# One broadcast matmul from doubled gate rows, and a last projection with the tokens on the partitions

## The chip, the cores and the metric

The program runs on one core of a Trainium2 chip. The metric is the device time of one execution in microseconds (us), from runs of the whole kernel; lower is better.

## The reference

Input and output are 512 tokens of 1024 features, all in float32. The first block normalises the tokens, projects them onto some 13,000 columns and feeds three branches: HGRN2 (8 heads), a stabilised mLSTM (4 heads) and Mamba-2 (16 heads in 4 groups). Each branch is multiplied by a sigmoid gate and its own output matrix, the sum goes through `w_out`, and a gated feed-forward layer with a short convolution follows. The second block has a gated convolution and a windowed attention of 8 heads. Two places matter for the change. In the mLSTM and in Mamba-2, rows over time enter an exponential for every pair of tokens t, s (here of Mamba-2):

```
cum = moveaxis(cumsum(dtc * A, axis=1), 1, 2)
L = exp(where(tri, cum[..., :, None] - cum[..., None, :], NEG_BIG))
y_intra = einsum('bhts,bshp->bthp', CB * L, xdt)
```

So a row of 512 numbers, one per token, has to stand on all partitions. The other place is the very end:

```
y = concatenate([y_conv, y_attn], axis=-1)
x = x + einsum('bse,ed->bsd', y, w_out)
return x
```

Here `y` has 4 tiles of 128 features from the convolution (numbers 0 to 3) and 4 from the attention (4 to 7).

## The kernel before

**Layout.** Activations lie with features on the partitions: a tile is 128 features by 512 tokens, and 8 tiles are the whole width. TensorE, the tensor engine, works on float32r operands, float32 rounded so that a matmul takes one pass; to keep float32 accuracy each operand is split into a high and a low part, and a product is three matmuls (high·high, high·low, low·high; L397, L398 and L399 in `project`). Weights come in 245 slabs of 512 KB, eight 128 x 128 blocks each. SyncE (SP) loads a slab into one of four buffers (L331) when `slab_used` says that its predecessor there has been used; ScalarE (ACT) writes its high part (`slab_hi`, L855); GpSimd (POOL) writes the low part over the raw slab (`slab_lo`, L362) and counts `slab_split`, for which TensorE waits. `project` takes one slab: 24 matmuls of 128 x 512 into one of two accumulator banks of PSUM (`acc`), in turn.

**Order.** Every engine runs a list of instructions written out by hand and waits on counting semaphores. The stages follow one another: HGRN2, the gate rows, four mLSTM heads, four Mamba-2 groups, mixing, feed-forward, attention with the gated convolution, and the last projection. Inside a stage TensorE alternates projections for the next unit with the small matmuls of the present one.

**The broadcast (`on_all`, L403 to L407).** The rows (Mamba-2's 16 heads in rows 0 to 15, the mLSTM's i and f in rows 32 to 35 and 64 to 67) are computed by VectorE (DVE) in `rows_part`, beside the projections of the first gates. The last steps split the row tile `r3` into `csh` (high) and `csl` (low, L1476), and copy two selection matrices to `selr` (L1465, L1466). `on_all(bank, c, sem)` takes column c of `selr`, repeated 128 times as the stationary operand, and runs two matmuls of 128 x 512, one with `csh` and one with `csl`, so that one row stands on all partitions of a bank. It is called 24 times: per mLSTM head once ahead of the exponentials (part 0, bank 5) and once behind the numerators (part 2, bank 2), and once per Mamba-2 head (`mb_bcast`, bank 5).

**A Mamba-2 group.** TensorE: `mb_start` transposes two tiles, multiplies B and C, and ends with the broadcast of head 0, which waits until `mb_rms` has read bank 5. Then for h = 0 to 3: a projection for the next group, the broadcast of head h + 1 (h < 3), and behind h = 1 and h = 3 the values of two heads (`mb_values`, L618). Two projections and `mb_finish` follow. DVE works through: the last normalisation of the group before (L1772, two), two tiles times dt (L1750), then per head four additions (`mb_head`, L1734), a convolution of four steps for the next group (L1503, L1508; from head 1 on, and not in the last group), and three products (`mb_weights`, L1744). ACT has the exponentials between them (L1092, L1093).

**The last projection, J_O2 = 237.** Slab 237 + f holds the columns of output feature tile f for all 8 input tiles. The first projection runs six of its blocks (input tiles 0, 1, 2, 4, 5, 6), then TensorE turns the last two rows of attention weights (`at_turn`, L771), computes the last values (`at_values`, L782; it waits for `at_copy` on ACT, L1285) and runs blocks 3 and 7, which wait for the low halves of those tiles: `cv_lo` (L2012), and `at_end`, `at_hi`, `at_lo` (L1972, L1289, L1977). DVE adds each finished bank to the residual `xT` (L2048); one projection later `turn_out` transposes the sum's four blocks (L833), ACT copies them (L1351) and SP stores them (L346): 128 features of all tokens, in runs of 512 bytes. Behind the last projection this chain stands alone. ACT's list there is `cv_silu`, two `at_copy`, `cv_hi`, `at_hi`, slab 240, then one slab and one copy in turn.

## Time and profile before

| | |
|---|---|
| Median of 3 runs | 1667.75 us (1667.38 to 1668.54) |
| The profiled execution's own time | 1668.24 us |
| Its span, first to last instruction | 1666.4 us |
| Instructions | 21787 |

A row of the timeline has the start in us, the duration (of the whole group, where it has several), the engine, the line of the kernel, the operation, output and inputs by name, shapes and count, and in brackets how long the engine sat idle and what released it. PEld is the loading of a stationary operand, PE the matmul. A matmul's duration is longer than the distance to the next start, since matmuls overlap; the distance is what it costs.

### The profile page before, as it was taken

How to read it: one execution, taken by the hardware profiler on the slowest of the kernel's cores; microseconds unless marked ns; L12 is line 12 of the kernel's file. 1: busy time of each engine (PE TensorE's matmuls, PEld its weight loads, DVE VectorE, ACT ScalarE, POOL GpSimd, SP SyncE). 2: the span in 40 equal slices, each digit the busy share in tenths (PEclk: the TensorE clock that was granted, in tenths of full speed). 3: DMA queues.
4: the chain of work that ended last, by engine and by line, in shares of the span. 5: the costliest groups of instructions: out<-in, count | busy, mean ns of one | idle time of the engine just before them, and what ended most of it. 6: DMA issues, size and time to landing. Idle time of an engine off the chain costs nothing.

```text
span 1666.4 us, 21787 instructions
## 1 busy us (share of the span) xinstructions
PE 1626.3 (98%) x7802; PEld 1303.4 (78%) x7802; DVE 855.5 (51%) x1329; ACT 723.4 (43%) x1143; POOL 607.8 (36%) x254
## 2 busy tenths in 40 slices
PE   7999999999999999999999999999999999999889
PEld 6888888777877778777777878888888877777667
DVE  4788878532454551167643335444443335565651
ACT  4656665332344432354554344444343333435441
POOL 5333223343333334332233434444444443242222
PEclk9999999999999999999999999999999999999999
DMA  5222112122222223222222322323233352222112
GB/s 185 65 64 64 63 63 64 54 88 89 87 76 76 66 75 101 76 76 64 64 76 82 95 89 93 96 89 99 88 101 102 101 178 88 64 76 68 59 51 89
DMA packets 41785, 139.31 MB, mean 84 GB/s; under 512 B 4200, under 2 KB 8552, under 8 KB 41712
## 3 DMA queue, kind: packets, MB, share of 16 engines
q1 hardware_dynamic: 40080, 132.66, 25.3%
q10 hardware_dynamic: 1632, 5.64, 0.9%
q8 instruction: 51, 0.84, 0.2%
q14 instruction: 22, 0.18, 0.0%
HBM read 136.15 MB, written 2.13 MB: 83 GB/s over the span
## 4 chain that ended last, share of the span: by engine, by line
PE 87%; DVE 6%; ACT 3%; issue 3%; DMA 0%; DVEq 0%; ACTq 0%; SPq 0%
PE bank L397 25%; PE bank L398 25%; PE bank L399 25%; PE bank L491 2%; PE bank L618 1%; PE bank L782 1%; PE bank L762 1%; DVE s_p L1744 1%; PE bank L771 1%; DVE unit L1508 1%; DVE hgd L1525 1%; DVE s_e L1734 0%; PE bank L588 0%; PE bank L508 0%; PE bank L539 0%
## 5 line engine op out<-in xcount | busy, mean ns | idle before, releaser
L362 POOL TENSOR_TENSOR wl<-raw,wh 128x1024 fp32r<-128x1024 f32 x245 | 599.6, 2449 | 1028.0 <-ACT wh L855 1027.7
L397 PE MATMUL bank<-hh,wh 128*128 128x512 f32 x968 | 390.2, 403 | 1.4 <-DVE hl L1977 1.0
L398 PE MATMUL bank<-hl,wh 128*128 128x512 f32 x968 | 382.9, 396 | 0.0
L399 PE MATMUL bank<-hh,wl 128*128 128x512 f32 x968 | 382.8, 395 | 0.0
L397 PE MATMUL bank<-yh,wh 128*128 128x512 f32 x800 | 320.9, 401 | 0.7 <-DVE yl L1779 0.5
L398 PE MATMUL bank<-yl,wh 128*128 128x512 f32 x800 | 317.0, 396 | 0.0
L399 PE MATMUL bank<-yh,wl 128*128 128x512 f32 x800 | 316.9, 396 | 0.0
L855 ACT ACTIVATE wh<-raw 128x1024 fp32r<-128x1024 f32 x241 | 253.2, 1054 | 110.8 <-DMA raw<-slabs 110.8
L397 PEld LDWEIGHTS bank<-hh,wh 128*128 128x128 f32 x968 | 182.1, 188 | 47.0 <-issue 4.1
L399 PEld LDWEIGHTS bank<-hh,wl 128*128 128x128 f32 x968 | 182.0, 188 | 44.3
L398 PEld LDWEIGHTS bank<-hl,wh 128*128 128x128 f32 x968 | 182.3, 188 | 42.0 <-issue 0.7
L397 PEld LDWEIGHTS bank<-yh,wh 128*128 128x128 f32 x800 | 150.8, 189 | 42.9 <-issue 6.2
L399 PEld LDWEIGHTS bank<-yh,wl 128*128 128x128 f32 x800 | 150.8, 189 | 36.7
L398 PEld LDWEIGHTS bank<-yl,wh 128*128 128x128 f32 x800 | 150.9, 189 | 35.5 <-issue 0.5
L1863 DVE TENSOR_TENSOR f_t<-bank,rsn 128x512 f32<-128x512 f32 x44 | 30.4, 692 | 121.5 <-PE bank L399 115.6
L397 PE MATMUL bank<-fh,wh 128*128 128x512 f32 x176 | 69.6, 396 | 0.0
L398 PE MATMUL bank<-fl,wh 128*128 128x512 f32 x176 | 69.6, 396 | 0.0
L399 PE MATMUL bank<-fh,wl 128*128 128x512 f32 x176 | 69.6, 396 | 0.0
L1525 DVE TENSOR_TENSOR hgd<-hg 128x512 f32<-128x512 f32 x56 | 67.2, 1200 | 0.0
L1834 DVE TENSOR_TENSOR xT<-xT,bank 128x512 f32<-128x512 f32 x16 | 11.0, 688 | 102.2 <-PE bank L399 102.2
L1331 ACT ACTIVATE a_l<-a_l,a_st 128x512 f32<-128x512 f32 x32 | 23.2, 725 | 88.7 <-DVE a_st L1956 88.7
L491 PEld LDWEIGHTS bank<-hgz 128*128 128x128 f32 x448 | 53.6, 192 | 7.8 <-issue 3.8
(304 smaller groups left out, 1874.7 us busy)
## 6 DMA issues: line engine op xcount, KB each, us to landing
raw<-slabs SPq DMA_DIRECT2D x245, 512.0 KB, 3.5
wb<-bias_scratch ACTq DMA_DIRECT2D x1, 3584.0 KB, 12.4
xs<-x SPq DMA_DIRECT2D x4, 512.0 KB, 6.1
out<-htn SPq DMA_DIRECT2D x8, 256.0 KB, 2.3
con<-consts ACTq DMA_DIRECT2D x1, 992.5 KB, 4.7
oneh<-onehot ACTq DMA_DIRECT2D x1, 512.0 KB, 5.6
con<-consts ACTq DMA_DIRECT2D x1, 192.0 KB, 4.6
par<-params ACTq DMA_DIRECT2D x1, 191.5 KB, 6.1
```

Source lines behind the costliest of these rows:

```text
L362: pool.tensor_tensor(slab(wl, i), slab(raw, i), slab(wh, i).bitcast(F32), ALU.subtract).then_inc(S["slab_split"], 1)
L397: mm(bank[:, :], wh[:, s, b, :], xh, start=first and i == 0, stop=False)
L398: mm(bank[:, :], wh[:, s, b, :], xl, start=False, stop=False)
L399: ins = mm(bank[:, :], wl[:, s, b, :], xh, start=False, stop=last and i == len(order) - 1)
L491: ins = mm(bank[:, b * P // 2:(b + 1) * P // 2], blk(z, b), right[:, b, :, :], start=True, stop=True)
L618: ins = mm(bank[64 * v:64 * v + 64, o:o + n], s_x[:, b, h + v, :], s_p[v][:, a:a + n], start=k == 0, stop=k == len(parts) - 1)
L762: ins = mm((b5, b6)[hd][:, :], a[r, q * P:(q + 1) * P], b[r, :], start=k == 0, stop=k == 2)
L771: ins = pe.transpose(blk((b2, b3)[i % 2], b), blk(a_l[i % 4], b), ident)
L855: A(wh[:, i].rearrange("p k f -> p (k f)"), raw[:, i].rearrange("p k f -> p (k f)"), ACT.Copy).then_inc(S["slab_hi"], 1)
L1331: A(a_l[i % 4][:, :], a_l[i % 4][:, :], ACT.Exp, bias=a_st[:, i, 0:1], accum_out=a_st[:, i, 1:2]).then_inc(S["at_ex"], 1)
L1525: TT(o, v, v[:, :, half - 1:half].broadcast_to([P, T // n, n]), ALU.subtract).then_inc(S["hg_d"], 1)
L1863: TT(f_t[v][:, :], acc[j0 % 2][:, :], rsn[:, :], ALU.mult).then_inc(acc_free[j0 % 2], 1)
```

## The change

Three things are changed.

**Doubled rows.** The gate weights' slab, their biases and constants hold each gate row a second time, 16 rows further down. DVE's last step makes one tile `cs`: its first copies hold -r3, its second copies the difference of the high part and r3. A selection column has -1 at both copies, so that one matmul sums both. The low part `csl`, the second selection matrix and the second matmul of `on_all` go. DVE has one small copy less.

**Token-major last projection.** The stationary operand is now a 128 x 128 block of `hh` or `hl` (128 tokens), the moving one two rows of a slab with 512 output columns. A slab holds two input tiles for half of the output columns. Per half (g) and block of 128 tokens (b), one bank takes first the four transposed residual tiles and then the 24 matmuls of four slabs on top. The order of the input tiles is (0, 1), (2, 4), (5, 6), (3, 7). TensorE runs: tile (0, 0); `at_turn` of rows 6 and 7; tile (0, 1); `at_values`; tile (0, 2); the wait for the last low halves; tile (0, 3); tiles (1, 0) to (1, 3).

**Leaving.** `turn_out` and DVE's additions are gone. ACT copies the banks of token blocks 0 and 2, DVE those of blocks 1 and 3, straight from PSUM, and SP stores each in runs of 2048 bytes. ACT does slab 240 ahead of `cv_hi` and `at_hi`.

```diff
             def on_all(bank, c, sem):
 
                 w = selr[:, c:c + 1].broadcast_to([P, P])
-                mm(bank[:, :], w, csh[:, :], start=True, stop=False)
-                mm(bank[:, :], w, csl[:, :], start=False, stop=True).then_inc(sem, 1)
+                mm(bank[:, :], w, cs[:, :], start=True, stop=True).then_inc(sem, 1)
...
-                    dve.tensor_copy(selr[:, 0:P], ident).then_inc(S["rnm_done"], 1)
-                    dve.tensor_copy(selr[:, P:2 * P], cc(K_SEL2)).then_inc(S["rnm_done"], 1)
+                    dve.tensor_copy(selr[:, :], cc(K_SEL2)).then_inc(S["rnm_done"], 1)
...
-                    TT(csl[:, :], r3[:, :], csh[:, :].bitcast(F32), ALU.subtract).then_inc(S["rnm_done"], 1)
+                    STT(cs[:, :], csh[:, :].bitcast(F32), cc(K_AGAIN, 1), r3[:, :], ALU.mult, ALU.subtract
+                        ).then_inc(S["rnm_done"], 1)
...
-            project(J_O2, src=(hh, hl), t0=J_O2 - DN_SHIFT, order=(0, 1, 2, 4, 5, 6), last=False,
-                    ready=[(sem, i) for sem in (S["cv_lo"], S["at_lo"]) for i in (1, 2, 3)])
+            def out_tile(g, i):
+
+                j = J_O2 + 4 * g + i
+                pe.wait_ge(S["slab_split"], j + 1)
+                w = [t[:, j % 4].rearrange("p k f -> p (k f)") for t in (wh, wl)]
+                for b in range(NB):
+                    bank = out_banks[g][b]
+                    if i == 0:
+                        out_free(g, b)
+                        for f in range(4):
+                            mm(blk(bank, f), blk(xT[:, 4 * g + f, :], b), ident, is_transpose=True, start=f == 0,
+                               stop=False)
+                    for n, k in enumerate(O2_PAIRS[i]):
+                        xh, xl = blk(hh[:, k, :], b), blk(hl[:, k, :], b)
+                        for c, (v, u) in enumerate(((xh, 0), (xl, 0), (xh, 1))):
+                            ins = mm(bank[:, :], v, w[u][:, n * T:(n + 1) * T], start=False,
+                                     stop=i == 3 and n == 1 and c == 2)
+                    if b == NB - 1:
+                        ins.then_inc(S["slab_used"], 1)
+                    elif i == 3:
+                        ins.then_inc(S["out_sum"], 1)
+
+            out_banks = ((acc[1], acc[0], b4, b5), (b6, b2, b3, b7))
...
+            out_tile(0, 0)
             at_turn(6, 3)
             at_turn(7, 3)
+            out_tile(0, 1)
             at_values(3, 3)
...
+            out_tile(0, 2)
+            pe.wait_ge(S["cv_lo"], 4)
+            pe.wait_ge(S["at_lo"], 4)
+            out_tile(0, 3)
+            for i in range(4):
+                out_tile(1, i)
...
+            slab_hi(J_O2 + 3)
             cv_hi(3)
             at_hi(3)
-            slab_hi(J_O2 + 3)
...
+            for g in range(2):
+                for b in (0, 2):
+                    act.wait_ge(S["out_sum"], 3 * g + b + 1)
+                    A(os_[g][b], (acc[1], None, b4, None, b6, None, b3)[4 * g + b][:, :], ACT.Copy
+                      ).then_inc(S["out_ev0"], 1)
+                    if g == 0 and b == 0:
+                        slab_hi(J_O2 + 7)
...
+            for g in range(2):
+                for b in (1, 3):
+                    if b == 3:
+                        dve.wait_ge(S["slab_used"], J_O2 + 4 * g + 4)
+                    else:
+                        dve.wait_ge(S["out_sum"], 3 * g + b + 1)
+                    dve.tensor_copy(os_[g][b], (None, acc[0], None, b5, None, b2, None, b7)[4 * g + b][:, :]
+                                    ).then_inc(S["out_ev1"], 1)
```

## Rows read from the trace of the kernel before

**Rows 1.** The page: busy time, and the shares of the chain that ended last.

```profile
PE 1626.3 (98%) x7802; PEld 1303.4 (78%) x7802; DVE 855.5 (51%) x1329; ACT 723.4 (43%) x1143; POOL 607.8 (36%) x254
...
PE 87%; DVE 6%; ACT 3%; issue 3%; DMA 0%; DVEq 0%; ACTq 0%; SPq 0%
```

**Rows 2.** Views of one line: L407 (ns least/median/most, first and last start), and L1362.

```profile
L407 PE MATMUL bank<-csl,selr x24: 388/392/400, 438.0 to 865.1; 128*128 128x512 f32 x24
...
L1362 DVE COPY xT<-bank x6: 682/685/692, 6.6 to 11.2; 128x512 f32<-128x512 f32 x6
```

**Rows 3.** Timeline, PE: a broadcast in group 1 of Mamba-2, and the values behind one in group 3.

```profile
762.43 0.40 PE L406 MATMUL bank<-csh,selr 128*128 128x512 f32 x1
762.66 0.39 PE L407 MATMUL bank<-csl,selr 128*128 128x512 f32 x1
763.57 1.63 PE L618 MATMUL bank<-s_p,s_x 128*64 128x384 f32 x14 [0.52 <-DVE s_p L1744]
...
856.81 0.87 PE L618 MATMUL bank<-s_p,s_x 128*64 128x384 f32 x4
```

**Rows 4.** Busy time by stretch (start:end, length, then each engine; PEclk the granted clock).

```profile
320.00:560.00 240.00, 240.00 (x1093) 192.88 (x1093) 97.62 (x145) 83.88 (x118) 83.99 (x36) 1.00 0.26 79
699.00:702.60 3.60, 3.09 (x15) 3.12 (x16) 1.38 (x2) 2.69 (x4) 0.00 (x0) 0.53 0.23 88
1576.00:1583.00 7.00, 6.21 (x20) 4.39 (x18) 5.91 (x12) 3.17 (x6) 2.38 (x1) 0.52 0.00 0
```

**Rows 5.** Timeline, mLSTM head 0: DVE's last sum, TensorE's first value matmul.

```profile
455.52 0.29 DVE L1690 TENSOR_TENSOR m_ps<-m_ps,m_p 128x128 f32<-128x128 f32 x1
...
458.07 0.81 PE L584 MATMUL bank<-m_p,m_v 128*128 128x384 f32 x2
```

**Rows 6.** Timeline, DVE in group 1, from the normalisation's end to its second products.

```profile
750.19 1.41 DVE L1772 SCALAR_TENSOR_TENSOR s_y<-s_y,par,s_rs 128x512 f32<-128x512 f32 x2 [6.22 <-ACT s_rs L1112]
...
761.91 1.60 DVE L1744 TENSOR_TENSOR s_p<-s_e,bank 128x512 f32<-128x512 f32 x3
```

**Rows 7.** Timeline, DVE: group 0, then head 3 of group 1, then group 3.

```profile
710.76 1.13 DVE L1734 SCALAR_TENSOR_TENSOR s_e<-bank,ncc,con 128x128 f32<-128x128 f32 x4 [1.07 <-PE bank L407]
...
772.26 1.13 DVE L1734 SCALAR_TENSOR_TENSOR s_e<-bank,ncc,con 128x128 f32<-128x128 f32 x4 [2.93 <-PE bank L407]
...
854.99 1.62 DVE L1744 TENSOR_TENSOR s_p<-s_e,bank 128x512 f32<-128x512 f32 x3 [2.25 <-ACT s_e L1093]
```

**Rows 8.** Timeline around the last attention values.

```profile
1608.74 0.50 PE L397 MATMUL bank<-hh,wh 128*128 128x512 f32 x1
...
1615.39 1.09 PE L782 MATMUL bank<-a_pt,a_v 128*64 128x128 f32 x16 [1.32 <-ACT a_pt L1285]
...
1618.69 0.50 PE L397 MATMUL bank<-hh,wh 128*128 128x512 f32 x1 [1.03 <-DVE hl L1977]
```

**Rows 9.** Timeline, the end: last matmul, transposes, the last sum, its way out.

```profile
1661.09 0.39 PE L399 MATMUL bank<-hh,wl 128*128 128x512 f32 x1
1661.32 0.60 PE L833 MATMUL bank<-con,xT 128*128 128x128 f32 x4
1661.64 0.69 DVE L2048 TENSOR_TENSOR xT<-xT,bank 128x512 f32 x1 [5.34 <-PE bank L399]
...
1662.58 1.49 SPq L346 DMA_DIRECT2D out<-htn  x2
1663.07 0.60 ACT L1351 ACTIVATE htn<-bank 128x512 f32<-128x512 f32 x1 [0.52 <-PE bank L833]
```

**Rows 10.** DMA issues of the page: KB each, median us from issue to landing.

```profile
raw<-slabs SPq DMA_DIRECT2D x245, 512.0 KB, 3.5
out<-htn SPq DMA_DIRECT2D x8, 256.0 KB, 2.3
```

**Rows 11.** Timeline, PE: a transpose group between two projections; float32 matmuls over a sum.

```profile
1655.28 0.60 PE L833 MATMUL bank<-con,xT 128*128 128x128 f32 x4
...
462.45 1.02 PE L591 MATMUL bank<-m_ps,con 128*128 128x512 f32 x2
```

More of the change, by code:

```diff
@@ L86 @@
 ROW_DT, ROW_I, ROW_F = 0, 32, 64
+AGAIN = 16
 W_BIAS = 896
@@ L311, in build @@
         rr, a_y = sqn
-        os_ = htn
+        os_ = [[t[:, :] for t in a_l], [au[0][:, b, :] for b in range(NB)]]
         OFF = {0: (512, 384), 2: (896, 128), 1: (1024, 256)}
@@ new lines, in _, with out_free @@
+            out_banks = ((acc[1], acc[0], b4, b5), (b6, b2, b3, b7))
+            def out_free(g, b):
+                if b == 0 and g == 0:
+                    pe.wait_ge(S["x2_done"], 9)
+                    pe.wait_ge(acc_free[1], (J_O2 - DN_SHIFT) // 2)
+                elif b == 1 and g == 0:
+                    pe.wait_ge(acc_free[0], (J_O2 - DN_SHIFT + 1) // 2)
+                elif b == 2 and g == 0:
+                    pe.wait_ge(S["at_v"], 4)
+                elif b == 3 and g == 0:
+                    pe.wait_ge(S["at_l"], 32)
@@ L822, in _ @@
+            out_tile(0, 0)
             at_turn(6, 3)
             at_turn(7, 3)
+            out_tile(0, 1)
             at_values(3, 3)
-            project(J_O2, src=(hh, hl), t0=J_O2 - DN_SHIFT, order=(3, 7), first=False,
-                    ready=[(S["cv_lo"], 4), (S["at_lo"], 4)])
-            def turn_out(f):
-                filled(pe, J_O2 - DN_SHIFT + f)
-                wait(pe, S["out_ev"], f - 3)
-                for b in range(NB):
-                    ins = pe.transpose(blk(psum[2 + f % 4], b), blk(xT[:, f, :], b), ident)
-                ins.then_inc(S["out_tr"], 1)
@@ L836, in _ @@
-            for f in range(1, KT):
-                project(J_O2 + f, src=(hh, hl), t0=J_O2 - DN_SHIFT + f)
-                turn_out(f - 1)
-            turn_out(KT - 1)
+            out_tile(0, 2)
[4 more added lines that the diff above has]
+                out_tile(1, i)
         @block.scalar
@@ L2041, in _ @@
             at_lo(3)
-            dve.wait_ge(S["x2_done"], 9)
-            with dve.Fori(0, KT // 4) as it:
-                for f in range(4):
-                    t = J_O2 - DN_SHIFT + f
-                    dve.wait_ge(S["slab_used"], it * 4 + (J_O2 + f + 1))
-                    fo = it * 4 + f
-                    TT(tile_of(xT, fo), tile_of(xT, fo), acc[t % 2][:, :], ALU.add).then_inc(acc_free[t % 2], 1)
+            for g in range(2):
+                for b in (1, 3):
[5 more added lines that the diff above has]
+                                    ).then_inc(S["out_ev1"], 1)
 def bucket(rel):
@@ L2066, in constants @@
     c[:, K_BD:K_BD + P] = (i[:, None] // AT_DH) == (i[None] // AT_DH)
-    for h in range(ML_HEADS):
-        c[ROW_I + h, K_SELI + ROW_I + h] = 1
-        c[ROW_I + h, K_SEL2 + h] = c[ROW_F + h, K_SEL2 + h] = 1
-        c[ROW_F + h, K_NSELF + ROW_I + h] = -1
+    for d in (0, AGAIN):
+        for h in range(MB_HEADS):
+            c[ROW_DT + d + h, K_SEL2 + ROW_DT + h] = -1
+        for h in range(ML_HEADS):
+            c[ROW_I + d + h, K_SELI + ROW_I + d + h] = 1
+            c[ROW_F + d + h, K_NSELF + ROW_I + d + h] = -1
+            c[ROW_I + d + h, K_SEL2 + ROW_I + h] = -1
+            c[ROW_I + d + h, K_SEL2 + ROW_F + h] = c[ROW_F + d + h, K_SEL2 + ROW_F + h] = -1
+    c[:, K_AGAIN] = i // AGAIN % 2
     c[:, K_CLAMP:K_CLAMP + P] = np.where(i[:, None] <= i[None], 0.0, NEG)
@@ L2103, in slabs_of @@
     for row, c, n in ((ROW_DT, C_MBDT, MB_HEADS), (ROW_I, C_MLIF, ML_HEADS), (ROW_F, C_MLIF + ML_HEADS, ML_HEADS)):
-        small[:, :, row:row + n] = w_in[:, c:c + n].reshape(KT, P, n).transpose(1, 0, 2)
+        for d in (0, AGAIN):
+            small[:, :, row + d:row + d + n] = w_in[:, c:c + n].reshape(KT, P, n).transpose(1, 0, 2)
     for u in range(HG_HEADS):
@@ L2122, in slabs_of @@
         put(J_O + f, i["w_out"][0], P * f)
-        put(J_O2 + f, i["w_out_2"], P * f)
         for c, n in enumerate(DN_CHUNKS):
             put(J_DN + 3 * f + c, w_dn, P * f, 8 * c, n)
+    for g in range(2):
+        for s, pair in enumerate(O2_PAIRS):
+            for n, k in enumerate(pair):
+                a[J_O2 + 4 * g + s].reshape(P, 2, T)[:, n] = i["w_out_2"][k * P:(k + 1) * P, g * T:(g + 1) * T]
     for j in range(NF):
```

50 lines of the change are left out of this document (23 added, 27 removed).

## The prediction

> **What bounds the kernel now.** I read the page first: TensorE is busy for 98% of the span, and the chain that ended last lies on it for 87% [rows 1]. Rows of single lines and of the timeline come next, because with such a share the question is not which engine bounds the kernel but where TensorE's list is what everybody waits for, and where it waits itself. In the busy times by stretch, 320 to 560 us, which holds mLSTM work, has TensorE busy for all of its 240 us [rows 4]: a matmul less there is time less. In Mamba-2 it is not always so: TensorE waits for DVE's products ahead of the values [rows 3]. At the end it waits twice around the last attention values [rows 8], and behind the last matmul a chain of DVE, TensorE, ACT and SP stands alone [rows 9].
>
> **The broadcast, unit price.** One matmul of 128 x 512 goes from each of 24 calls [rows 2]. It lasts 0.39 us, but the next one starts 0.23 us after it [rows 3], and this distance is what it occupies. All 24 are 5.5 us. A page's rule gives another price: the Trainium skill, "TensorE: Matmul & The Clock Gate", section "Back-to-back issue gap", has 512 / 2.4 + 2.5 = 216 ns for one. By it, 24 would be 5.2 us, and what I count below as 3.5 us would be 3.2. The trace disagrees, and its distance is used.
>
> **The broadcast in the mLSTM.** Eight calls. TensorE has no idle time there [rows 4], and the nearest wait has room: in head 0 DVE's last sum ends at 455.81, and the first value matmul starts at 458.07 [rows 5]. Two calls per head take less than 0.5 us out of that room of 2.3 us, and what follows a call starts earlier too. So 8 x 0.23 = 1.8 us.
>
> **The broadcast in Mamba-2, group by group.** In group 1, DVE goes from the end of the normalisation at 750.19 to its second products, which end at 761.91 + 1.60 = 763.51 [rows 6]. On the way it waits for ACT alone. TensorE issues three broadcasts in this time, and then waits for the products and starts at 763.57 [rows 3]. Three matmuls less bring TensorE there 0.7 us earlier, to the same wait: worth nothing, the idle 0.5 us becomes 1.2. Group 2 has the same list of work, so the same. In group 3, without convolutions, DVE's second products end at 854.99 + 1.62 = 856.61 [rows 7] and TensorE starts the values at 856.81 [rows 3]. With the 0.06 us that group 1 shows between end and start, 0.14 us is left to win of 0.7. In group 0 nothing of a group before holds DVE: it waits for the broadcast, at 710.76 [rows 7]. There broadcasts 0 and 1 count in full; of broadcast 2 I take 0.1, between 0 and 0.23. The fourth broadcast of every group counts, since DVE waits for it (2.93 us in group 1 [rows 7]), and TensorE and what it waits for move together. Mamba-2 is then 0.56 + 0 + 0 + 0.14 + 4 x 0.23 = 1.6 us. Both together give **3.5 us**. The ends are 1.8 (no more than the mLSTM) and 5.5.
>
> **The rows themselves.** The doubled columns use slab columns that the projection multiplies anyway; one step of DVE changes its form, and one copy goes. All of it lies beside projections in a stretch in which TensorE has no idle time [rows 4]: nothing. If that cover were gone, it would be a small copy gained.
>
> **The last projection, TensorE.** From 1608.74 to the transposes at 1661.32 are 52.6 us [rows 8, 9]. One projection and one group of four transposes take 1661.32 - 1655.28 = 6.04 us [rows 9, 11], of which 24 x 0.233 = 5.60 are matmuls and 0.44 transposes. Eight projections and the six groups within the stretch are 8 x 6.04 - 2 x 0.44 = 47.4 us; the two turns, eight transposes, are 0.9, the values (1.09 of duration [rows 8], less the overlap) 1.0. That leaves 52.6 - 49.3 = 3.3 us in which TensorE waits or refills, of which the rows name 1.32 and 1.03. The new order puts 5.6 us of matmuls between the turns and the values, and again between the values and the wait for the last low half. Before, that second wait ends 1618.69 - 1616.48 = 2.2 us behind the values [rows 8]: 5.6 covers it, even with a slab ahead of `cv_hi` on ACT, which only delays a tile that is needed a whole out tile later. I take 3.0 of the 3.3 us, and 0.3 stays as refill. Against it stand 0.87 us: all 32 transposes are now ahead of the last matmul, before only 24. Number and distance of the matmuls stay: blocks of 128 x 128 stationary, 512 columns moving, both ways. So the last matmul starts 2.1 us earlier.
>
> **The way out.** Before, from the last matmul at 1661.09: DVE starts 0.55 later, adds for 0.69, TensorE turns, ACT copies until 1663.07 + 0.60 = 1663.67 [rows 9]. Now DVE copies from PSUM, 0.685 us [rows 2], and is done 0.55 + 0.69 = 1.24 behind it instead of 2.58: 1.3 us. The last store is of 256 KB as before; it took 2.3 us to land, and a slab, twice as large in runs eight times as long, 3.5 [rows 10]. Longer runs then give between nothing and 0.55 us (half of a slab's time, as if there were no fixed part); I take nothing, because the out row itself is the nearest. By the Trainium skill ("DMA: Bandwidth & Descriptors", "Why small descriptors are slow"), each packet costs three cycles beside its 32-byte beats; by that the move to 2048 bytes would save some 0.1 us, not shown by any row here.
>
> **Supply and queues.** SP's list has the same slabs; slab 241 may be loaded when tile (0, 0) is done, which is earlier than before, and is needed 18 us later. ACT's slabs 241 to 243 sit behind `at_hi`, and its first copy behind slab 243; that copy delays only stores of the first half, with 20 us left. DVE has nothing else. The banks that tile (0, 0) takes are free by the time it comes to them: the last is bank 5, which DVE reads for two logits, of about the 0.69 us of its addition [rows 9] each with a reduction between, while blocks 0 to 2 take 3 x (0.44 + 6 x 0.233) = 5.5 us. The end is worth 2.1 + 1.3 = **3.5 us** (rounded once).
>
> **Sum.** 3.5 + 3.5 = 6.9 us with the decimals kept. The profiled execution took 1668.24 us with a span of 1666.4; it becomes 1661.3. It lies 0.5 us above the median, so from the median of 1667.75 I say **1660.8**.
>
> **Rivals.** The difference from no change that a measurement of this kernel can tell is 0.2%, 3.3 us.
>
> *All broadcasts count.* If DVE's chain in Mamba-2 shortened as well, 5.5 in place of 3.5: 1658.8. Against it, the chain of group 1 waits for nothing of TensorE's [rows 6]. 8%.
>
> *The end keeps its stalls.* If the order or a bank held TensorE as before: 3.0 less, 1663.8. For it, out tile (0, 0) now waits for two more banks; against it, their readers are done. 6%.
>
> *No broadcast counts*, since other waits take their place in the mLSTM and in group 0 too: 1664.3. Against it, the full 240 us [rows 4]. 8%.
>
> *The clock.* TensorE was granted half its 2.4 GHz, 1.2 GHz, in two places: 0.53 on average of 3.6 us behind its wait at the start of Mamba-2, and 0.52 over 7 us behind the waits in the attention [rows 4]. Group 1 and 2 now wait 1.2 us instead of 0.5. One more stretch like the first costs 3.6 x 0.47 = 1.7 us: 1662.5. Against it, waits of 1.3 us did not bring the clock down at 1615 [rows 8]: TensorE's distances stay at 0.23 behind it. 9%.
>
> *Nothing visible*, no broadcast counts and the stalls stay: 1667.3. That the change doesn't do what it says ends here too, if the doubled rows only shifted the waits. 5%.
>
> *Slower: the matmuls of the last projection take longer.* Its place is the 192 matmuls onto a bank that a transpose has opened, with the weights as the moving operand. From 6.9 / 192 = 0.036 us more for each, the gain is gone. The nearest dearer row is float32 matmuls of the same shape, two in 1.02 us of duration [rows 11], some 0.43 each, 0.20 more: 192 x 0.20 = 38 us, 1699. Against it, both operands stay float32r, and a matmul behind transposes keeps its distance but for the 0.44 counted. 3%.
>
> **How the numbers follow.** My forecast has 61%, and the predicted time is its own. The range is to hold 8 in 10: forecast, all broadcasts, the clock and the stalls, with 0.6 us to both sides for the scatter of the runs (1667.38 to 1668.54). It is 1658.2 to 1663.9, and leaves out the three others, 16%. Faster by over 0.2% (below 1664.4) are the forecast and the first four rivals: 0.92. Within 0.2%: 0.05. Slower: 0.03.
>
> **What would show it.** Right: 24 rows of one broadcast matmul; the first values of groups 1 and 2 still start 13.4 us behind the normalisation's end, with 1.2 us idle ahead; no wait above 0.3 us from 1608 on; the last copy ends 1.2 us behind the last matmul's start. Wrong: idle time in the mLSTM stretch, a distance other than 0.233 us in the last projection, a wait for a slab there, or a stretch with a lower clock where there was none.

## The result, and the profile after

| | before | after |
|---|---|---|
| median of 5 runs, us (lowest to highest) | 1667.38 (1664.79 to 1668.54) | 1657.11 (1656.43 to 1659.72) |
| profiled execution, us (span; mean granted clock) | 1668.24 (1666.4; 0.994) | 1656.43 (1654.4; 0.997) |

The ratio is 0.9944, with a 95% interval of 0.9932 to 0.9955: faster by over 0.2%, as forecast, but 1657.11 is 3.7 us under the number and 1.1 us under the range of the forecast.

The page of the kernel after: busy times and the chain, to be held against [rows 1], then the two stores of the output, against [rows 10].

```profile
PE 1617.4 (98%) x7778; PEld 1296.2 (78%) x7778; DVE 854.2 (52%) x1324; ACT 721.7 (44%) x1139; POOL 605.9 (37%) x254
...
PE 87%; DVE 6%; ACT 3%; issue 3%; DMA 0%; DVEq 0%; ACTq 0%; SPq 0%
...
out<-a_l SPq DMA_DIRECT2D x4, 256.0 KB, 4.1
out<-au SPq DMA_DIRECT2D x4, 256.0 KB, 2.0
```

TensorE has 24 matmuls less, the chain is where it was. The stores of the first half land behind slab traffic in 4.1 us, which nobody waits for; those of the second half in 2.0 us, before 2.3.

Timeline of TensorE in groups 1 and 3 of Mamba-2, against [rows 3], and of DVE in group 1, against [rows 6].

```profile
757.70 0.40 PE L408 MATMUL bank<-cs,selr 128*128 128x512 f32 x1
759.18 1.08 PE L619 MATMUL bank<-s_p,s_x 128*64 128x384 f32 x6 [1.08 <-DVE s_p L1773]
...
851.84 0.87 PE L619 MATMUL bank<-s_p,s_x 128*64 128x384 f32 x4 [0.35 <-DVE s_p L1773]
```

```profile
745.79 1.42 DVE L1801 SCALAR_TENSOR_TENSOR s_y<-s_y,par,s_rs 128x512 f32<-128x512 f32 x2 [6.21 <-ACT s_rs L1139]
```

From the start of the normalisation's last step (which the forecast calls its end) to the first values it is 759.18 - 745.79 = 13.39 us; before 763.57 - 750.19 = 13.38. Three matmuls of the broadcasts are gone in between, and TensorE waits 1.08 us instead of 0.52; the forecast had 1.2.

Busy time by stretch (columns as in [rows 4]).

```profile
320.00:560.00 240.00, 240.00 (x1093) 192.90 (x1092) 97.18 (x144) 84.21 (x118) 85.09 (x36) 1.00 0.25 79
697.00:700.60 3.60, 3.19 (x23) 2.90 (x24) 1.29 (x2) 2.59 (x4) 0.00 (x0) 1.00 0.20 79
1569.80:1576.80 7.00, 7.00 (x38) 5.20 (x37) 6.07 (x12) 3.19 (x6) 2.41 (x1) 0.76 0.00 0
```

The mLSTM still has no idle time. But the second stretch has the full clock, where [rows 4] had 0.53, and the third 0.76 instead of 0.52. That is not a matter of instructions: r1_after below has the same ones, and a low clock there.

Timeline of the end, in two pieces: the last turns and the subtraction in DVE that was late before; the last values, and the last matmul with its way out, against [rows 8, 9].

```profile
1601.71 0.48 PE L836 MATMUL bank<-wh,hh 128*128 128x512 f32 x1
...
1608.66 1.04 PE L772 MATMUL bank<-con,a_l 128*128 128x128 f32 x8
...
1611.88 2.48 DVE L2041 TENSOR_TENSOR hl<-c,hh 128x512 fp32r<-128x512 f32 x1 [4.23 <-ACT hh L1324]
```

```profile
1614.82 0.40 PE L836 MATMUL bank<-wl,hh 128*128 128x512 f32 x1
1615.14 1.09 PE L783 MATMUL bank<-a_pt,a_v 128*64 128x128 f32 x16
1616.16 0.51 PE L836 MATMUL bank<-wh,hh 128*128 128x512 f32 x1
...
1650.84 0.40 PE L836 MATMUL bank<-wl,hh 128*128 128x512 f32 x1
1651.27 0.69 DVE L2077 COPY au<-bank 128x512 f32<-128x512 f32 x1 [2.06 <-PE bank L836]
1651.99 0.33 SPq L350 DMA_DIRECT2D out<-au  x1
```

Both waits of [rows 8] are gone, and the last copy ends 1651.96 - 1650.84 = 1.12 us behind the last matmul's start. DVE's low half took 2.48 us, beside POOL's split of a slab; TensorE had the rest of a tile, the values and another tile ahead of needing it.

**The difference by stretch.** I took fixed matmuls as marks (the same one in every kernel, near the named time in the profile of before) and worked out from their starts how much shorter than in the profile of before each stretch is, in us. All profiles of this study are in it.

```
                    to     to     to     to     to     to     to     last   last   span's
                    300    407    608    689    729    889    1567   scores matmul end     sum
after             -0.21  -0.01  -1.87   0.00  -2.31  -0.79  -0.21  -2.05  -2.81  -1.80  -12.1
r1_after          -0.52   0.02  -1.87   0.00  -0.87  -0.85  -0.17  -0.01  -2.81  -1.81   -8.9
r2_after           0.90   1.02  -1.87   0.00  -2.18  -0.86   0.20  -0.87  -2.80  -1.80   -8.3
e1_bcast           0.63  -0.02  -1.87   0.00  -2.19  -0.85   0.06  -2.08   0.01   0.00   -6.3
e2_tail            0.70  -0.01   0.00   0.00   0.33   0.01  -0.23  -1.22  -2.81  -1.80   -5.0
e3_xdt            -0.51   0.02  -1.87   0.00  -0.56  -3.66   0.06  -2.05  -2.80  -1.79  -13.2
e4_order          -0.63   0.01  -1.87   0.00  -0.72  -0.87   0.16  -0.26   4.39  -1.80   -1.6
e5_runs           -0.30  -0.01  -1.87   0.00  -0.57  -0.86   0.06  -0.17  -2.81  -1.18   -7.7
e6_same           -0.32   0.01  -1.87   0.00  -0.71  -0.83   0.16  -0.17  -2.81  -1.81   -8.3
e8_fill            0.09  -0.03  -1.87   0.00  -2.50  -0.79   0.23  -2.07  -2.02  -1.80  -10.7
e7_early           0.93   0.99  -1.87   0.73  -5.31  -3.65  -0.12   0.09  -2.81  -1.80  -12.8
e7_again           0.41  -0.02  -1.87   0.73  -5.29  -3.65   0.13  -1.36  -2.81  -1.80  -15.5
e9_best            0.86  -0.03  -1.87   0.00  -5.29  -3.66   0.18  -0.86  -2.80  -1.80  -15.3
```

Columns in which kernels with the same code differ (to 300, 407, 729, the last scores) are those in which TensorE's clock falls to half. Where the code is the same, the others repeat within 0.1 us, but for the seventh, which varies by 0.5.

### The profile page after: what moved, and what is told of

Its sections match the earlier page's. It is cut to its first block, busy times and chain, and to the rows that moved or that the text cites. A ratio compares the mean times of both kernels' runs of the same rounds, so it can differ in the third digit from the quotient of the medians.

```text
span 1654.4 us, 21691 instructions
## 1 busy us (share of the span) xinstructions
PE 1617.4 (98%) x7778; PEld 1296.2 (78%) x7778; DVE 854.2 (52%) x1324; ACT 721.7 (44%) x1139; POOL 605.9 (37%) x254
## 4 chain that ended last, share of the span: by engine, by line
PE 87%; DVE 6%; ACT 3%; issue 3%; DMA 0%; DVEq 0%; ACTq 0%; SPq 0%
PE bank L399 24%; PE bank L401 24%; PE bank L400 24%; PE bank L836 3%; PE bank L492 2%; PE bank L619 1%; PE bank L783 1%; PE bank L763 1%; DVE s_p L1773 1%; PE bank L772 1%; DVE unit L1537 1%; DVE s_e L1763 1%; DVE hgd L1554 1%; PE bank L589 0%; PE bank L509 0%
## 5 line engine op out<-in xcount | busy, mean ns | idle before, releaser
L399 PE MATMUL bank<-hh,wh 128*128 128x512 f32 x904 | 364.4, 403 | 0.2 <-DVE unit L1537 0.2
L401 PE MATMUL bank<-hh,wl 128*128 128x512 f32 x904 | 357.6, 396 | 0.0
L400 PE MATMUL bank<-hl,wh 128*128 128x512 f32 x904 | 357.4, 395 | 0.0
L399 PEld LDWEIGHTS bank<-hh,wh 128*128 128x128 f32 x904 | 170.3, 188 | 42.7 <-issue 4.2
L401 PEld LDWEIGHTS bank<-hh,wl 128*128 128x128 f32 x904 | 169.9, 188 | 41.4
L400 PEld LDWEIGHTS bank<-hl,wh 128*128 128x128 f32 x904 | 170.4, 188 | 39.7 <-issue 0.7
```

The lines of the kernel that those rows point to most:

```text
L399: mm(bank[:, :], wh[:, s, b, :], xh, start=first and i == 0, stop=False)
L400: mm(bank[:, :], wh[:, s, b, :], xl, start=False, stop=False)
L401: ins = mm(bank[:, :], wl[:, s, b, :], xh, start=False, stop=last and i == len(order) - 1)
```

## The experiments

Each took its turn with the kernel before on the same chip. The kernel before gave medians of 1668.03 (11 runs), 1667.71 (15), 1667.33 (9) and 1666.88 (9) beside the four series.

**e1_bcast: the doubled rows and the one broadcast alone.** The last projection is that of the kernel before.

```diff
 def on_all(bank, c, sem):
-    mm(bank[:, :], w, csh[:, :], start=True, stop=False)
-    mm(bank[:, :], w, csl[:, :], start=False, stop=True)
+    mm(bank[:, :], w, cs[:, :], start=True, stop=True)
```

> Only the doubled rows and the single broadcast matmul; the last projection as before. Theory (TensorE's own wait in three Mamba-2 groups swallows half of the saving): 3.5 us less than before at the same number of low-clock stretches, the wait ahead of the first values of groups 1 and 2 grows from some 0.7 to 1.25 us start to start, group 3 from none to 0.5. Rival 1 (every removed matmul counts): 5.5 us less. Rival 2 (the extra gain of the whole change beyond the 6.9 us forecast comes from here): 4.5 us or more less, with new differences elsewhere in the rows.

Measured 1661.95 us (1660.78 to 1662.34, 5 runs), ratio 0.9962 [0.9948, 0.9976]. By the medians that is 6.1 us, more than the theory's 3.5 and in the reach of both rivals; but its runs had a mean clock of 0.9962 beside 0.9948, some 2.3 us by that difference alone, so the medians decide nothing here. By stretch it has 1.87 in the mLSTM and 0.85 in groups 1 to 3, and nothing at the end. 2.19 in group 0 and 2.08 in the attention hold clock. From the last broadcast's start to the first values, groups 1 and 2 now have 1.47 us instead of 0.91, and group 3 0.75 instead of 0.32, in the trace: the waits have grown, as the theory had it.

**e2_tail: the token-major projection alone.** Two matmuls per broadcast as before; the last projection is that of the kernel after.

```diff
-for f in range(1, KT):
-    project(J_O2 + f, src=(hh, hl), t0=J_O2 - DN_SHIFT + f)
-    turn_out(f - 1)
+for i in range(4):
+    out_tile(1, i)
```

> Only the token-major last projection; the broadcast with two matmuls as before. Theory: from the scores' last matmul to the end of the program 4.6 us less than before, against the 3.5 us forecast: 2.8 us up to the last matmul (3.0 of waits, 0.75 from a distance of 229 in place of 233 ns over 192 matmuls, less 0.87 for two transpose groups moved ahead of it) and 1.8 us behind it. Rival (the end was sized rightly and the clock made the rest): 3.5 us.

Measured 1663.36 us (1660.68 to 1664.71, 7 runs), ratio 0.9973 [0.9961, 0.9984]. The last projection gives 2.81 us and the way out 1.80, together 4.61 (theory 4.6, rival 3.5), and there is nothing at all in the stretches of the broadcasts. The two parts do not touch each other.

**r1_after: the kernel after once more.**

> The changed kernel once more, for more executions beside their granted clock. Theory (what lies beyond 3.5 + 4.6 = 8.1 us is the clock): executions with a mean clock of 0.997, 0.996 and 0.995 lie about 1.5 us apart each, and at the same clock the change is worth 8.1 us. Rival (the change itself keeps the clock up): the kernel before never shows as high a clock as this one.

Measured 1657.99 us (1656.91 to 1659.53, 5 runs), ratio 0.9939 [0.9925, 0.9952]. Its profiled execution shows what the first one hid: the same instructions as the kernel after, but the clock low where the kernel before has it.

```profile
698.40:701.80 3.40, 3.40 (x12) 2.68 (x12) 0.46 (x1) 0.70 (x1) 0.00 (x0) 0.53 0.02 5
1572.00:1579.00 7.00, 6.36 (x18) 4.60 (x19) 5.65 (x11) 3.16 (x6) 2.37 (x1) 0.51 0.00 0
```

With low stretches of the same lengths as before, but for the very end, the span is 1666.44 - 1657.56 = 8.9 us shorter. The other 3.2 us of the first profile, 1657.6 - 1654.4, are 1.44 (group 0) and 2.04 (attention) of clock, less 0.3 elsewhere. Over all 15 runs of this code (the five of r2_after below included) those with a clock of 0.995, 0.996 and 0.997 average 1659.5, 1657.3 and 1656.4 us: 2.2 and 0.9 apart, where 1.5 each was expected. The rival as it was put is out: the kernel before reached 0.997 too, in 4 of 35 runs.

**e3_xdt: what did hold TensorE in groups 1 and 2.** If three broadcasts are worth nothing since DVE's chain is longer, taking something out of that chain must be worth its full time. DVE's product of values and step sizes, which only the values need, goes behind the first head's sum.

```diff
 for g in range(MB_GROUPS):
-    mb_xdt(g)
     for h in range(5):
         if h < 4:
             mb_head(g, h)
+        if h == 0:
+            mb_xdt(g)
```

> The changed kernel with one step of VectorE moved: in every Mamba-2 group the two products of tiles with dt come behind the first head's four additions, into the time in which ScalarE has the exponentials, instead of ahead of them. Theory (the wait ahead of the first values is VectorE's and ScalarE's chain from the end of the normalisation, which the removed matmuls cannot shorten): the chain is about 1.05 us shorter, the first values of groups 1 and 2 start 1.05 us earlier, those of group 3 about 0.5, 2.6 us less than the changed kernel in all. Rival (the wait is for the broadcast or for something else of TensorE's): no change, within 0.5 us.

Measured 1654.77 us (1654.40 to 1656.70, 5 runs), ratio 0.9924 [0.9910, 0.9937]. Groups 1 to 3 give 3.66 us instead of 0.85, 2.8 more. Timeline of DVE in group 1: the product (L1779) now stands behind the sum (L1763), and the products (L1773) follow without the wait for ACT that the kernel after has there.

```profile
747.27 1.41 DVE L1801 SCALAR_TENSOR_TENSOR s_y<-s_y,par,s_rs 128x512 f32<-128x512 f32 x2 [6.21 <-ACT s_rs L1139]
748.60 1.12 DVE L1763 SCALAR_TENSOR_TENSOR s_e<-bank,ncc,con 128x128 f32<-128x128 f32 x4
749.64 1.27 DVE L1779 TENSOR_TENSOR s_x<-bank,dtc 128x512 f32<-128x512 f32 x2
750.84 1.28 DVE L1808 TENSOR_TENSOR yl<-s_y,yh 128x512 fp32r<-128x512 f32 x2
752.04 1.60 DVE L1773 TENSOR_TENSOR s_p<-s_e,bank 128x512 f32<-128x512 f32 x3
```

The same rows in r1_after: from the normalisation to the products it is 752.83 - 746.94 = 5.89 us with 1.04 of waiting, here 752.04 - 747.27 = 4.77.

```profile
746.94 1.41 DVE L1801 SCALAR_TENSOR_TENSOR s_y<-s_y,par,s_rs 128x512 f32<-128x512 f32 x2 [6.22 <-ACT s_rs L1139]
...
752.83 1.62 DVE L1773 TENSOR_TENSOR s_p<-s_e,bank 128x512 f32<-128x512 f32 x3 [1.04 <-ACT s_e L1120]
```

**e4_order: no tile between turns, values and waits.**

```diff
 at_turn(6, 3)
 at_turn(7, 3)
-out_tile(0, 1)
 at_values(3, 3)
-out_tile(0, 2)
 pe.wait_ge(S["cv_lo"], 4)
 pe.wait_ge(S["at_lo"], 4)
+out_tile(0, 1)
+out_tile(0, 2)
```

> The kernel after the change, with the first three tiles of the last projection put behind the last attention turn's transposes and values instead of between them: the refill and waits of before should come back. The stalls of the page before (1.48 us ahead of the values, 0.41 and 1.19 us ahead of the next matmuls in the timeline) return in part: my theory says the last matmul starts 2.2 to 3.1 us later than in the kernel after the change (waits of about 1.5 us ahead of the last values and 0.7 to 1.6 us ahead of the next tile's first matmul), way out unchanged at about 3.4 us behind it. Rival: the gain of the end came from the form of the matmuls alone; then less than 0.5 us.

Measured 1666.42 us (1664.00 to 1667.04, 10 runs), ratio 0.9988 [0.9978, 0.9997]: 8.4 us of 10 are given back, and my 2.2 to 3.1 was far off. The edit moves two tiles; the first, (0, 0), stays ahead of the turns, other than the expectation says. Timeline of TensorE around the values; of ACT, POOL and DVE; then the clock.

```profile
1613.70 1.09 PE L783 MATMUL bank<-a_pt,a_v 128*64 128x128 f32 x16 [0.74 <-ACT a_pt L1312]
1619.65 0.76 PE L836 MATMUL bank<-wh,hh 128*128 128x512 f32 x1 [4.85 <-issue]
```

```profile
1613.54 1.06 ACT L882 ACTIVATE wh<-raw 128x1024 fp32r<-128x1024 f32 x1
1614.67 2.34 POOL L364 TENSOR_TENSOR wl<-raw,wh 128x1024 fp32r<-128x1024 f32 x1 [8.65 <-ACT wh L882]
1615.14 2.42 DVE L2041 TENSOR_TENSOR hl<-c,hh 128x512 fp32r<-128x512 f32 x1 [4.21 <-ACT hh L1324]
1617.48 0.68 DVE L2001 TENSOR_TENSOR sqn<-bank,au 128x512 f32<-128x512 f32 x1
1618.86 0.69 DVE L2006 TENSOR_TENSOR hl<-sqn,hh 128x512 fp32r<-128x512 f32 x1 [0.69 <-ACT hh L1316]
```

```profile
1616.40:1623.20 6.80, 3.55 (x9) 2.86 (x10) 2.45 (x3) 1.58 (x2) 2.98 (x2) 0.52 0.01 2
```

The slow subtraction of 2.4 us, which nothing waited for in the kernel after, now stands ahead of the last head's chain, and TensorE waits 4.85 us. In the kernel before the same point came 2.2 us behind the values [rows 8], and its own subtraction had no split of POOL beside it:

```profile
1615.89 0.69 DVE L2012 TENSOR_TENSOR hl<-c,hh 128x512 fp32r<-128x512 f32 x1 [0.80 <-ACT hh L1297]
```

The difference of 2.7 us is, by these rows, the change's slab ahead of `cv_hi`: some 1 us of ACT, and 2.42 - 0.69 = 1.7 us more of DVE beside POOL's split. In this wait the clock falls to half, for 6.8 us, where the kernel after has the full clock; the ten runs have a mean clock of 0.9934, those of the kernel after 0.9957. By stretch, 4.39 + 2.81 = 7.2 us: 0.8 for the values (see e8_fill), 4.85 of wait, and 1.6 that are left for the clock, against half of the 3.5 us of it in which TensorE worked. The rival, that the order is worth nothing, is out.

**e8_fill: only the first of the two tiles moved.**

```diff
 at_turn(7, 3)
-out_tile(0, 1)
 at_values(3, 3)
+out_tile(0, 1)
 out_tile(0, 2)
```

> The kernel after the change with one tile moved: the second tile of the last projection stands behind the last attention values instead of between transposes and values; the waits for the last heads' rows stay ahead of the fourth tile. Theory: the tile only covered the copy of the transposed probabilities (0.90 us in the three heads before), so 0.9 us more and no stall of 5 us, since two tiles still stand ahead of the wait that cost it. Rival: any change of that order brings ACT's and DVE's chain to the end of the cover, and over 2 us come back.

Measured 1657.79 us (1657.63 to 1660.07, 4 runs), ratio 0.9950 [0.9935, 0.9965]. By TensorE's timeline it waits once, for ACT's copy, and the last matmul comes 0.79 us later than in the kernel after (-2.02 against -2.81), a tenth under the theory.

```profile
1609.18 1.04 PE L772 MATMUL bank<-con,a_l 128*128 128x128 f32 x8
1610.95 1.09 PE L783 MATMUL bank<-a_pt,a_v 128*64 128x128 f32 x16 [0.74 <-ACT a_pt L1312]
```

**e5_runs: stores in runs of 512 bytes.** Both sides of each store take the four pieces of 128 columns in reversed order, so that they can't be joined.

```diff
-sp.dma_start(out...[:, b, g * T:(g + 1) * T], os_[g][b])
+sp.dma_start(out...[:, b, g * T:(g + 1) * T].rearrange("p (f c) -> p f c", f=4)[:, ::-1, :],
+             os_[g][b].rearrange("p (f c) -> p f c", f=4)[:, ::-1, :])
```

> The kernel after the change, with the four 128-column pieces of every output row stored in reversed order on both sides, so that each transfer of 256 KB moves in runs of 512 bytes as before instead of 2048; the output is the same. Theory (longer runs land sooner): the last transfer lands in about 2.3 us instead of 2.0, end 0.3 us later. Rival (the landing time differs only because other transfers had ended): 2.0 us as in the kernel after, no difference.

Measured 1659.90 us (1657.76 to 1660.73, 4 runs), ratio 0.9946 [0.9931, 0.9961]. The medians are too near to tell; the page's row of the DMA issues does:

```profile
out<-au SPq DMA_DIRECT2D x4, 256.0 KB, 2.6
```

2.6 us to land instead of 2.0, and the way out is 0.6 us longer. The size is over my 2.3, and not all of it is the transfer: landing is counted from the start of the issue, and SP's issue itself takes 0.60 us here, 0.33 in the kernel after.

```profile
1655.71 0.60 SPq L350 DMA_DIRECT2D out<-au  x1
```

Of its own form the kernel before had 2.3, so the change itself has 0.3 from this. The rival, that landing was sooner only because other transfers had ended, is out.

**e6_same: another order within the three products.**

```diff
-for c, (v, u) in enumerate(((xh, 0), (xl, 0), (xh, 1))):
+for c, (v, u) in enumerate(((xh, 0), (xh, 1), (xl, 0))):
```

> The kernel after the change, with the three products of each pair in the last projection in the order high by high, high by low, low by high, so that two follow each other with the same stationary activations. Theory A (the 229 ns between starts come from the form, activations stationary and weight columns moving, whatever the order): 229 ns, no change. Theory B (it depends on what follows what, since the three pairs gave 231.7, 227.5 and 229.2 ns): the pair with the same stationary operand is nearer 216 to 225 ns, and the 192 matmuls take 0.3 us or more less. Theory C (the same stationary costs more): over 233 ns.

Measured 1659.74 us (1659.34 to 1660.28, 4 runs), ratio 0.9949 [0.9934, 0.9964], and the last projection again 2.81 us shorter than before. The durations of L836, in the view of one line, first of the kernel after, then here:

```profile
L836 PE MATMUL bank<-wh,hl x64: 388/388/398, 1602.0 to 1650.6; 128*128 128x512 f32 x64
L836 PE MATMUL bank<-wl,hh x64: 392/392/397, 1602.3 to 1650.8; 128*128 128x512 f32 x64
```

```profile
L836 PE MATMUL bank<-wl,hh x64: 388/388/398, 1605.8 to 1654.3; 128*128 128x512 f32 x64
L836 PE MATMUL bank<-wh,hl x64: 392/392/397, 1606.0 to 1654.6; 128*128 128x512 f32 x64
```

388 and 392 ns stay with the second and third place and do not go with the operand. The distances do the same: 231.6, 227.3 and 229.5 ns in places one to two, two to three, three to one, as before 231.7, 227.5 and 229.2. So 229 ns is a matter of the form (theory A), and a stationary operand used twice in a row saves nothing.

**e7_early: the wait ahead of the clock's stretch at 699 us.** On top of e3_xdt, the six Silu activations of the first Mamba-2 group go ahead of the gates' loop on ACT, and one wait on TensorE goes behind the products that don't need it.

```diff
 def gates(b, j0):  # ACT
     act.wait_ge(S["ml_lo"], 2 * ML_HEADS)
+    mb_silus(0, range(6))
...
-silu_tables()
-mb_silus(0, range(6))
...
 def mb_start(g):  # TensorE
-        pe.wait_ge(S["g_acc"], KT)
...
+    if g == 0:
+        pe.wait_ge(S["g_acc"], KT)
     mb_bcast(g, 0)
```

> The kernel of the third run (values' factor behind the first head's work on DVE), with the six Silu activations of the first Mamba-2 group moved ahead of the gates' loop on ACT, and TensorE's wait for the last gate sum moved from ahead of this group's transposes to behind its C by B products. The stall of 3.0 us ahead of those transposes (697.14 in that profile, start to start 3.29 us) should go. Theory 1 (every low stretch of TensorE's clock past the start follows a stall of about 3 us): the stretch near 699 is gone as well, in every execution; time 2.5 to 3.0 us less for the stall and 1.4 us less wherever the stretch was there, so 3.0 to 4.4 us below that kernel (about 1651), mean clock 0.001 higher. Theory 2 (the stretches come by chance, not from the stall): 2.5 to 3.0 us less and a stretch near 699 in some profiles. Rival 3: the wait only moves on to the first broadcast or the values: under 1 us less.

Measured 1653.15 us (1651.39 to 1655.65, 5 runs), ratio 0.9910 [0.9897, 0.9924], 1.6 us below e3_xdt, not 3.0 to 4.4. The stretch up to 729 us is 5.31 instead of 0.56 us shorter, so wait and low clock are both gone there. Two things take of it. ACT's first Tanh of the gates comes later, and TensorE waits for it, 0.73 us in the column to 689. And in this profile three other low stretches were long: 6.8 us at the start, at 316 and at 1568 us.

**r2_after and e7_again: both once more, side by side.**

> The kernel after the change once more, for its executions' clocks and beside the next two. So far ten of its executions had a mean clock of 0.9957 and 26 of the kernel before 0.9947. If the change itself leaves the clock low for less time, it lies 0.0005 to 0.0015 above the kernel before again; if that was chance, they are equal and the median is about 1.2 us higher than so far.

> The kernel with the early Silu activations once more, beside the kernel after on the same chip. In its first profile the stall and the low stretch at 699 us were gone (4.0 us less between two fixed matmuls), but three other stretches were 6.8 us long instead of 3.4. If that was chance, its profile here has no stretch near 699 and the others as often short as long, mean clock at or over that of the kernel after, and the median is 5.5 to 7 us below the kernel after's. If low time only moves elsewhere, the clock is again below it and the difference 4.5 to 5 us.

r2_after: 1659.88 us (1655.90 to 1660.24, 5 runs), ratio 0.9948 [0.9934, 0.9961]. Its mean clock was 0.9956 beside 0.9954 of the nine runs of the kernel before: the kernel after repeated the 0.9957 of its first ten runs, but the kernel before, at 0.9947 until then, was as high here. The median is higher, as the second case had it, yet at the same mean clock: by the means the five are 0.7 us over the first ten. e7_again: 1652.89 us (1651.36 to 1654.29, 5 runs), ratio 0.9915 [0.9902, 0.9929]. It lies 7.0 us below r2_after, at a mean clock of 0.9960. The second profile of the early kernel has the 5.29 us again, no low clock at 699, and short stretches at 317 and 1567. TensorE's rows in it: the wait that came, and the transposes (L634) that follow a matmul at once, where e3_xdt had 2.89 us of waiting.

```profile
617.31 0.47 PE L399 MATMUL bank<-hh,wh 128*128 128x512 f32 x1 [0.49 <-ACT tg L1202]
...
691.82 0.40 PE L400 MATMUL bank<-yl,wh 128*128 128x512 f32 x1
...
695.55 0.39 PE L401 MATMUL bank<-yh,wl 128*128 128x512 f32 x1
695.78 1.03 PE L634 MATMUL bank<-con,unit 128*128 128x128 f32 x8
```

```profile
697.24 1.06 PE L635 MATMUL bank<-con,unit 128*128 128x128 f32 x8 [2.89 <-ACT unit L1125]
```

The second row is of e3_xdt, from its timeline. r2_after, with the kernel after's code, shows a third way in its busy times by stretch: full clock at 697 to 700.6, but 0.55 over 7.5 us from 315.5.

```profile
315.50:323.00 7.50, 6.30 (x20) 5.41 (x21) 5.29 (x13) 2.96 (x6) 2.53 (x1) 0.55 0.00 2
697.00:700.60 3.60, 0.92 (x9) 0.95 (x10) 2.14 (x3) 3.57 (x8) 1.47 (x1) 1.00 0.53 146
```

**e9_best: four activations early, two late.**

```diff
-    mb_silus(0, range(6))
+    mb_silus(0, range(4))
...
 gates(1, J_G1)
+mb_silus(0, (4, 5))
 exp_tables()
```

> The kernel with the early Silu activations, with four of the six ahead of the gates' loop (those that the transposes and products wait for) and the last two behind it. In the two profiles with all six, ACT's first Tanh of that loop came 4 us later than without them and TensorE stood 0.65 to 0.73 us at 619 us for its accumulator. Theory: with four, 2.1 us of ACT, that new wait is gone and the table load for the first head's exponentials is hidden by the transposes and products: 0.7 us less, median near 1652.2. Rival: the two activations and the table load behind the loop now hold up the first head's exponentials and give it back: no difference, or slower.

Measured 1652.16 us (1650.96 to 1654.07, 5 runs), ratio 0.9911 [0.9897, 0.9924]. The wait at 617 is gone (0.00 in the column to 689), and the 5.29 us stay: ACT's table load at 695.84 ends long before the first exponential at 700.18.

```profile
694.69 1.13 ACT L1126 ACTIVATE unit<-unit 128x512 f32<-128x512 f32 x2
695.84 1.28 ACT L877 ACT_TABLE_LOAD   x1
700.18 1.66 ACT L1120 ACTIVATE s_e<-bank,dend 128x128 f32<-128x128 f32 x6 [3.06 <-DVE s_e L1764]
```

It is the fastest kernel here, 14.7 us under the kernel before and 5.8 under the median of the 15 runs of the kernel after. That it beats e7_early by the 0.7 us is shown by the column, not by the medians.

## Why the prediction was right or wrong

Three steps failed, all on the same side: the distance of the matmuls in the last projection (0.7 us), the way out (0.5), and the clock, which the sum left as it was (1.1 to 1.5 us by all runs). The broadcasts and the waits went as forecast.

**The broadcast, 3.5 us: right.** The mLSTM gave 1.87, forecast 1.84. Groups 1 to 3 gave 0.79 to 0.87, forecast 0.14 and three times 0.23, which is 0.83. Group 0 gave 0.56 to 0.87 in the five profiles with the clock low at 699 as before; forecast 0.79. With their mean of 0.69 it is 3.4 us. Group 0 is the least certain of these: e2_tail, with the broadcasts and the low stretch of the kernel before, differs from it by 0.33 us there. That three broadcasts each in groups 1 and 2 are worth nothing shows in TensorE's wait, 1.08 for 0.52 us, and in e3_xdt, where the same groups give 2.8 us as soon as DVE's chain is shorter.

**The last projection on TensorE, 2.1 us: 0.7 too little.** The step that failed here is "Number and distance of the matmuls stay". The number did; the distance did not. Two rows of the last projection, twelve starts apart, from the timeline of the kernel after:

```profile
1610.01 0.39 PE L836 MATMUL bank<-wl,hh 128*128 128x512 f32 x1
...
1612.76 0.39 PE L836 MATMUL bank<-wl,hh 128*128 128x512 f32 x1
```

2.75 / 12 = 0.229 us. Sixteen starts of another projection, the rows 691.82 to 695.55 of e7_again above, give 3.73 / 16 = 0.233. The mean over the 192 is 229.4 ns against 233.3 ns, and 192 x 3.9 = 0.75 us. That is the difference to 2.81. It is so in all twelve profiles with this form. The Trainium skill, "TensorE: Matmul & The Clock Gate", section "Back-to-back issue gap", has 216 ns, as the gap of an isolated matmul, and about 131 ns for a stream of matmuls with their weight loads. The trace disagrees with both, for either form. The waits went as forecast: with 0.75 of 2.81 from the distance, 2.06 are left for the 2.1 of the sum. The last low half, for which tile (0, 3) waits, comes 2.2 us behind the values in the kernel after as before, and the tile between them, 24 x 0.229 = 5.5 us, covers it with 3.3 us to spare, nearly the 3.4 that I had worked out:

```profile
1617.70 0.69 DVE L2006 TENSOR_TENSOR hl<-sqn,hh 128x512 fp32r<-128x512 f32 x1 [0.70 <-ACT hh L1316]
```

That takes the other tile too, which stands ahead of the values and gives DVE time for the slow subtraction. Without it the last low half comes 4.85 us behind the values (e4_order), and one tile would cover that with 0.7 us to spare. The step "only delays a tile that is needed a whole out tile later", of the slab ahead of `cv_hi`, overlooked what the slab does to DVE; the order hid it.

**The way out, 1.3 us: 0.5 too little.** It gave 1.80. "I take nothing" for the longer runs was the wrong end of 0 to 0.55: landing took 2.0 for 2.3 us, and e5_runs takes it to 2.6. The rule on packets that I quoted from the Trainium skill ("DMA: Bandwidth & Descriptors", "Why small descriptors are slow") has the right sign, and my estimate by it was 0.1, a third of what was measured. The rest is that DVE starts 0.43 and not 0.55 behind the last matmul, and a few hundredths behind the landing.

**The clock: priced one way only.** This is what carried the result out of the range. The rival "The clock" has one stretch more and none less; the sum keeps the low stretches of the profile before as they are, without a reason. It also names two of them, where that profile has four ahead of the last matmul: at 16 and at 317 us the clock was at half for 3.4 us each, beside the two of [rows 4]. The change's own part is 3.4 + 2.8 + 1.8 = 8.0 us. With that in place of 6.9, the forecast would have been 1659.7, inside the range; the other 2.6 us down to 1657.11 are clock and the scatter of five runs.

The 15 runs of the kernel after average 1658.18 us, and 35 runs of the kernel before, those beside e1_bcast, e4_order and r2_after, 1667.64: 9.5 us. Series by series, against the kernel before beside it, it is 8.9, 9.9 and 8.5. So 1.1 to 1.5 us are beyond the 8.0, and they go with the clock: 0.9957 on average against 0.9949. 0.0008 of 1660 us are 1.3 us, some four fifths of what 3.4 us at half clock take (1.7); by the columns such a stretch costs 1.0 (at 316) to 2.1 us (the second in the attention).

Every low stretch in these profiles, up to the last matmul, begins in a wait of TensorE of 2.4 to 4.9 us or within 2.1 us behind it, and the one place that lost its wait (e7_early, e7_again, e9_best) had the full clock in all three profiles. With the wait there, seven of eleven had it low. Which of the places it is, and whether for 3.4 or 6.8 us, changes between executions of the same code. Three of the five runs first seen of the kernel after had 0.996 or 0.997, and the median of all its 15 is 1657.99, 0.9 us above 1657.11 and 0.2 under the range. (The upper end of the range has a slip: by its own rule, the stalls' 1663.8 and 0.6 more, it is 1664.4, not 1663.9. Nothing hangs on it.)

**Open.** Whether the change leaves the clock higher in itself, or 15 executions happened so: 0.0010 over the kernel before in the first ten, 0.0002 in the last five. Nor do three profiles with the full clock prove that the missing wait is the reason, where four of eleven had it with the wait; by that share, three in a row come by luck about one time in twenty. The early kernels, whose code excludes one stretch, have 0.9957 too in ten runs (e7_early, e7_again), no more than the kernel after, so that fewer waits do not simply mean a higher mean. Their median is 5.1 us under that of the kernel after, of which columns account for 2.8 and, without clock, some 2.2 (the wait of 2.9 less the new 0.7). What decides the length of a stretch wasn't found.

**The rivals.** The end's stalls did not stay; both waits are gone. "All broadcasts count" would have its 1658.8 near the result, and for the wrong reason: the columns exclude it, as they exclude "No broadcast counts" and "Nothing visible", by the 1.87 us of the mLSTM. The matmuls with the weights moving were dearer in my slower rival, and cheaper on the chip.

## What to carry to other kernels

When an engine is full, price a removed instruction by the distance between starts, and then look for the stretches where it waits anyway: there the price is zero, and the chain that it waits for is worth more than the instruction (2.8 us for one reordered step in each of three groups, against 0.9 for twelve removed matmuls). Before comparing two profiles by their spans, split them at fixed instructions: four columns of ten held all of the clock's noise, and the rest repeated within 0.1 us, one of them within 0.5. Where the clock falls in a wait of some microseconds or right behind it, its price is more than its length, and small work put into its cover saves both (e4_order: 7.2 us for two tiles' place).

## What the runs showed of the hardware

- A float32r matmul of 128x512 followed the one before it after 229.4 ns on average with the activations stationary and the weights moving, and after 233.3 ns the other way about, in every profile of either form (twelve and two); neither the order of the three products nor using a stationary operand twice running changed it. Why was not found.
- Within a triple of products the places had their own distances, 231.7, 227.5 and 229.2 ns in the kernel after, whatever the operands (e6_same); four other profiles (r1_after, e2_tail, e5_runs, e7_early) had 229.5, 228.4 and 230.5, with the same mean.
- A transfer of 256 KB out of SBUF landed in 2.0 us in runs of 2048 bytes, in 2.3 and 2.6 us in two forms of 512 bytes (of the 2.6, the issue itself took 0.60, in the runs of 2048 bytes 0.33), and in 4.1 us beside slab loads.
- A DVE subtraction of 128x512 took 2.42 to 2.49 us beside POOL's split of a slab on the same SBUF, and 0.69 us elsewhere (L2006, and L2012 before). In all twelve profiles in which the two overlap, it began 0.5 us behind the split and ended 0.54 to 0.55 us behind the split's end.
